# Retrieval's one-hot compares on VectorE: from tensor-tensor to scalar-tensor-tensor instructions

## The reference

```python
q = (xb @ w_q).reshape(nb, 8, 2, 64)
s1 = einsum('nhd,hkd->nhk', q[:, :, 0], keys1)      # 128 first keys
s2 = einsum('nhd,hkd->nhk', q[:, :, 1], keys2)      # 128 second keys
v1, i1 = top_k(s1, 16);  v2, i2 = top_k(s2, 16)
cand = v1[..., :, None] + v2[..., None, :]
sc, sel = top_k(cand, 16)                           # 16 experts a head
idx = take_along_axis(i1 * 128 + i2, sel)
g = softmax(sc)
h = einsum('nd,nhkd->nhk', xb, u[idx])
a = gelu(h) * g
return einsum('nhk,nhkd->nd', a, v[idx])
```

## Time and profile before

| | |
|---|---|
| median of 3 runs | 4929.05 us (4917.19 to 4929.27) |
| the profiled execution's own time | 4900.19 us |
| its span | 4898.4 us |
| VectorE busy, of the span | 3165.0 us, 65% |
| GpSimd busy | 626.6 us, 13% |
| one tile of `spread` and `choose` | 109.96 us (first compare of one tile at 2056.35, of the next at 2166.31) |
| compares for `bare`, 96 | 676 ns shortest, 2314 ns median |
| compares for `left`, 96 | 1208 ns shortest, 1211 ns median |

### The profile page before, as it was taken

How to read it: one execution, slowest core, us unless ns; L and a number is a source line. 1 busy time by engine, 2 the same in 40 slices (tenths; PEclk the granted TensorE clock), 3 DMA queues, 4 the chain that set the end, 5 groups by cost and what they waited for, 6 DMA issues and landing times. The chain is left out here.

```text
span 4898.4 us, 61601 instructions
## 1 busy us (share of the span) xinstructions
PE 4146.3 (85%) x20219; PEld 3468.1 (71%) x20219; DVE 3165.0 (65%) x5709; ACT 1272.6 (26%) x2699; POOL 626.6 (13%) x505
## 2 busy tenths in 40 slices
PE   6999798998887875355542899999999999999996
PEld 5788565875444665254442788999999999999995
DVE  4301343111111209999997789999999999999986
ACT  3111232111111211244433222222222222222222
POOL 0000000000000000133333211111111111111110
PEclk9999676556999977688877899999999999999998
DMA  4322321002004010011222777877877778777774
GB/s 137 114 90 79 90 59 39 19 19 89 31 26 155 0 39 5 5 73 73 90 116 94 271 272 269 281 280 271 281 272 272 281 277 280 276 275 286 273 269 168
DMA packets 308268, 770.86 MB, mean 157 GB/s; under 512 B 29121, under 2 KB 170945, under 8 KB 257729
## 3 DMA queue, kind: packets, MB, share of 16 engines
q0 software_dynamic: 55360, 403.60, 22.2%
q1 hardware_dynamic: 233376, 356.77, 21.8%
q10 hardware_dynamic: 19440, 9.44, 0.7%
HBM read 681.01 MB, written 89.78 MB: 157 GB/s over the span
## 5 line engine op out<-in xcount | busy, mean ns | idle before, releaser
L2078 PE MATMUL exp_h<-exp_xh,exp_uh 128*128 128x384 f32 x2048 | 690.5, 337 | 57.5 <-DVE exp_xl L2048 47.5
L2080 PE MATMUL exp_h<-exp_xh,exp_ul 128*128 128x384 f32 x2048 | 688.6, 336 | 0.0
L2079 PE MATMUL exp_h<-exp_xl,exp_uh 128*128 128x384 f32 x2048 | 687.8, 336 | 0.0
L2092 PE MATMUL exp_y<-exp_vh,exp_ah 128*128 128x512 f32 x1536 | 599.2, 390 | 10.5 <-DVE H L1983 10.5
L1900 POOL DMA_INDIRECT exp_uv<-in_peer_uv,gidx x384 | 374.1, 974 | 1795.4 <-DVE H L2010 1757.3
L2094 PE MATMUL exp_y<-exp_vh,exp_al 128*128 128x512 f32 x1536 | 601.6, 392 | 0.0
L2093 PE MATMUL exp_y<-exp_vl,exp_ah 128*128 128x512 f32 x1536 | 601.3, 391 | 0.0
L2004 DVE SCALAR_TENSOR_TENSOR exp_uv<-exp_uv,exp_gx 128x1024 f32<-128x1024 f32 x384 | 469.4, 1223 | 92.6 <-DMA exp_uv<-in_peer_uv,gidx 69.5
L2010 DVE SCALAR_TENSOR_TENSOR H<-exp_uv,exp_coef,H 128x1024 f32<-128x1024 f32 x384 | 491.1, 1279 | 24.0 <-ACT exp_coef L1945 24.0
L1983 DVE TENSOR_TENSOR H<-H,exp_y 128x512 f32<-128x512 f32 x768 | 490.0, 678 | 4.0 <-PE exp_y L2094 3.9
L1936 ACT ACTIVATE exp_ah<-exp_prod 128x384 fp32r<-128x384 f32 x256 | 132.4, 517 | 1353.0 <-DVE exp_prod L1993 1353.0
(11 more groups left out here) (276 smaller groups left out, 6285.5 us busy)
## 6 DMA issues: line engine op xcount, KB each, us to landing
exp_u<-in_peer_u SPq DMA_DIRECT2D x128, 512.0 KB, 4.9
exp_v<-in_peer_v SPq DMA_DIRECT2D x128, 512.0 KB, 4.1
exp_w<-s_w SPq DMA_DIRECT2D x128, 384.0 KB, 3.7
out_z<-proj_zs SPq DMA_DIRECT2D x72, 256.0 KB, 2.0
proj_w<-in_w_in SPq DMA_DIRECT2D x16, 1024.0 KB, 5.5
merge_gates<-out_z SPq DMA_DIRECT2D x9, 1024.0 KB, 5.1
s_zt<-proj_zt ACTq DMA_DIRECT2D x27, 256.0 KB, 2.3
exp_uv<-in_peer_uv,gidx POOLq DMA_INDIRECT x384, 5.7
```

The costliest lines, as they stand in the source:

```text
L2078: pe.matmul(hp[c][:, 0:TC], uh[s][:, n, :], xh[:, n, at], start=(n == 0), stop=False)
L2079: pe.matmul(hp[c][:, 0:TC], uh[s][:, n, :], xl[:, n, at], start=False, stop=False)
L2080: last = pe.matmul(hp[c][:, 0:TC], ul[s][:, n, :], xh[:, n, at], start=False, stop=(n == KD - 1))
L2092: pe.matmul(yp[x][:, :], ah[a + n][:, rows], vh[half][:, n, :], start=(n == 0), stop=False)
```

## The change

Both compares are issued as `scalar_tensor_tensor`, which computes (in0 `op0` scalar) `op1` in1. With `op0` a multiplication by the constant 1.0, the result is the same. Inputs, outputs, types, waits and semaphores stay as they are, and so do the number and the order of the instructions on every engine.

```diff
-                        dve.tensor_tensor(bare[r][:, :, :], key_of[:, :, :], over(key2t[:, bass.ds(b * OH, OH)], NKEY),
-                                          ALU.is_equal).then_inc(bare_ready, 1)
+                        dve.scalar_tensor_tensor(out=bare[r][:, :, :], in0=key_of[:, :, :], scalar=1.0,
+                                                 in1=over(key2t[:, bass.ds(b * OH, OH)], NKEY),
+                                                 op0=ALU.mult, op1=ALU.is_equal).then_inc(bare_ready, 1)
...
-                        dve.tensor_tensor(left[r][:, :, :], over(iota[:, :], OH), along(key1t[:, bass.ds(b * OH, OH)], NKEY),
-                                          ALU.is_equal).then_inc(left_ready, 1)
+                        dve.scalar_tensor_tensor(out=left[r][:, :, :], in0=over(iota[:, :], OH), scalar=1.0,
+                                                 in1=along(key1t[:, bass.ds(b * OH, OH)], NKEY),
+                                                 op0=ALU.mult, op1=ALU.is_equal).then_inc(left_ready, 1)
```

## The result

The change makes the kernel slower: 4962.19 us (median of 5 runs, 4952.06 to 4970.56) against 4921.52 (median of 5, 4917.19 to 4929.27), a ratio of 1.0087 with a 95% interval of 1.0067 to 1.0107. That is 41 us, with an interval of 33 to 53.

A forecast was written before the change was run, and what follows sets the result against it. VectorE, partly standing still for GpSimd, was taken to bound Retrieval's `spread`. A tile loses 2.2 + 6.05 = 8.2 us, six tiles 49, which on the median of 4929 gives 4978 us; range 4922 to 4996.

The forecast's parts named there:

- the one called likeliest: Retrieval: `bare` slows and still excludes GpSimd, so every batch lengthens; +49 us, 4978 us on the median, chance 0.77.
- the lost pace: The compare `bare` in bf16 drops from double to single pace in the new form, 0.68 to 1.22 us, +0.54.
- the exclusion: A compare with two SBUF inputs and GpSimd's multiply exclude each other, whichever starts first, in the new form too.
- the period: Time of one batch in the steady part of `spread`, said to go from 3.38 to 3.93 us.
- `left` costs 0.01 a batch: The f32 compare `left` goes from 1211 to at most 1225 ns, +0.01 us; +0.07 kept as the bound.
- a rival at 0.12: The new form doesn't contend with GpSimd, so the kernel gets faster: 4880 us, chance 0.12.
- The start of a tile: First batches of a tile, partly absorbed by idle time: `bare(4)` ends 2.1 to 2.3 us later, 2.2 in the sum.
- The steady part: Batches 5 to 15 of a tile, eleven compares behind `bare(4)`: 11 x 0.55 = 6.05 us a tile.
- The end of a tile: Adds nothing: `left(14)`, GpSimd's last scaling and `left(15)` keep their order and lengths.
- The sum on the median: Whole kernel: the median of 4929 us plus 49 gives 4978 us.
- The first rival: New form neither waits for GpSimd nor holds it up: 8.5 us a tile saved, 50 in all, chance 0.12.
- The third rival: Two SBUF sources halve the pace: `left` takes about 2.29 us, some 150 us more, 5080 us, chance 0.03.

The follow-up runs named there:

- e_left: Only the compare `left` put in the scalar-tensor-tensor form, against the kernel before; ratio 1.0005 (0.9984 to 1.0026).
- e_f32: Both compares kept as tensor-tensor, `key2t` held in f32 in place of bf16, against the kernel before; ratio 1.0096 (1.0064 to 1.0128).
- e_pool1_stt: Changed kernel with GpSimd's multiply cut from six tokens a batch to one, which alters the output; ratio to before 0.9853 (0.9811 to 0.9896).
- e_lpsum_stt: Changed kernel with `left` reading its second input from PSUM in place of SBUF; ratio to before 0.9978 (0.9959 to 0.9997).
- e_bare: Only the compare `bare` put in the scalar-tensor-tensor form, against the kernel before; ratio 1.0099 (1.0064 to 1.0134).
- e_lpsum: Kernel before, compares still tensor-tensor, with `left` reading its second input from PSUM in place of SBUF; ratio 0.9902 (0.9868 to 0.9937).

## Why the prediction was right

The time lay in the range, and the case that came is the one called likeliest, +41 us (33 to 53) where it said +49. Its three steps, the lost pace, the exclusion and the period, each came as described; the sizes were a little large.

- *`left` costs 0.01 a batch.* It costs nothing: 1211 to 1212 ns, and e_left is within 0.2 us of before over the stretch. It would have taken some 2.2 to 2.3 us at half the pace. The Trainium skill's rule that two SBUF sources other than bf16 halve this instruction's throughput (Vector Engine (DVE) Microarchitecture Reference, Points that are easy to get wrong) does not hold for it here; the measurement decides.
- *`bare` goes from 0.68 to 1.22 us, by the f32 rows of the same instruction.* Measured 1.21. e_f32 shows by another way that this is the single pace. The Trainium skill's list of packed operations (Vector Engine (DVE) Microarchitecture Reference, section 5.1 Performance modes) leaves scalar-tensor-tensor out, and the trace agrees: 1209 ns at the shortest, with all three operands in bf16.
- *The new form excludes GpSimd as the old one does.* This was argued from two inputs in SBUF, with no row of the new form, and a rival at 0.12 hung on it. e_left, e_pool1_stt and e_lpsum_stt show it. By the Trainium skill (SBUF — State Buffer, section SBUF: two separate sides) it takes two SBUF inputs on VectorE's side and a GpSimd operation that reads SBUF; all three agree, and with one input in PSUM `left` stays at 1.22 us or less. No run here has a GpSimd operation that doesn't read SBUF.
- *Where it lies.* The period is 3.90 us for 3.93 said, and a tile takes 117.77 for 118: VectorE enters the first tile's `spread` at 2077.53 and the sixth's at 2666.37, five tiles. Before it was 109.84 in the same way (2056.20 to 2605.39).
- *The start of a tile* was sized well: 1.90 us in the first tile and 2.1 in the mean of the six, for 2.2 said. The steady part was over-sized by a little: 11 x 0.53 = 5.8 in place of 11 x 0.55 = 6.05. A tile loses 7.9 by the terms and by the trace, for 8.2 said. Six times 7.9 is 47, and the stretch says 47.2.
- *The end of a tile* did not always keep its order, as was said: in two of the six tiles `left(15)` now starts just before GpSimd's last scaling and isn't held. `spread` is 1.3 us shorter there, but the next `choose` begins later behind it (1.8 us, seen in one of the two, since the other is the last tile). That hardly counts in the sum.
- *The sum on the median.* I added it to 4929, a median of three; two further runs put before at 4921.52. That is 7.5 of the 16 us by which 4978 was too high. The other 6 us between 47 and the timed 41 lie within the interval; e_bare, with the same stretch, timed at 47. What the rest of the kernel does in an execution isn't steadier than that, and no run shows a share of it that the change moves.
- *Slips that change nothing.* VectorE is at 9 tenths in slices 18 to 21 and at 7 in slice 22. The first rival's terms, 8.2 less 1.08 plus 1.6, are 8.7 a tile and 52 us, not 8.5 and 50. The third rival's slope of 1.04 ns a column is 0.99 by the rows that the prediction itself uses, which makes its `left` 2.23 us.

## What to carry to other kernels

Look at the shortest duration of an instruction against its median: here 676 against 2314 ns said that seven tenths of the compare were standing still for GpSimd. What is added to such a compare can then land wholly behind GpSimd's end, as it did here (1.08 us in place of 0.55). Changing the form of an instruction between equals isn't free if the old form ran packed and the new one doesn't. Where VectorE and GpSimd work in turns on SBUF, moving one input to PSUM, if it lies there anyway, was worth more (1.5%, and 1.8% with the work shifted) than the double pace that it cost.

## What the runs showed of the hardware

- Where a compare of VectorE with two SBUF inputs met a GpSimd multiply that reads SBUF, one of them stood still, at the single pace (2837 ns in the median where 1209 is the shortest) and at the double pace (2314 where 676 is). With one of the inputs in PSUM (1205 to 1224 ns, within 15 ns of the single pace from SBUF) they ran side by side.
- Reading one f32 column again and again from PSUM, as `left` does, costs nothing over SBUF: 1208 ns in the median in e_lpsum, 1211 before.
- One f32 input of two takes the whole instruction to the single pace, 1209 ns against 676, though the other input and the output are bf16 (e_f32).
